# Input sums held back, keys between the norm's parts, MLP loads later and two of four weight sums on GpSimd, in a float32 hybrid decoder layer

## The chip, the cores and the metric

One core of a Trainium2 chip runs one launch. The metric is device time in microseconds; the kernel before took 1165.41 us, the median of three runs.

## The reference

One decoder layer in float32 over 1024 tokens of width 1024, cut to its computation:

```python
mod = silu(c) @ w_ada + b_ada
shift1, scale1, gate1, shift2, scale2, gate2 = split(mod, 6)
h = rms_norm(x) * (1 + scale1) + shift1
gq, gk, gv, g_lr, g_gate, hq, hf, hi, h_gate = split(h @ w_in)
# four GLA heads, four HGRN2 heads, causal, chunks of 64 tokens:
#   o_t = q_t S_t,  S_t = diag(exp(log_a_t)) S_{t-1} + k_t^T v_t
o_gla  = rms_norm(gla(gq, gk, gv, log_sigmoid(g_lr @ w2 + b2) / 16), g1) * silu(g_gate)
forget = lb + (1 - lb) * sigmoid(hf)
o_hgrn = rms_norm(gla(silu(hq), 1 - forget, hi, log(forget)), g2) * silu(h_gate)
x = x + gate1 * (concat(o_gla, o_hgrn) @ w_out)
h = rms_norm(x) * (1 + scale2) + shift2
x = x + gate2 * (square(relu(h @ w_mlp1)) @ w_mlp2)
out = rms_norm(x, final_norm_g)
```

## The kernel before

Each engine's program is one list of instructions, and semaphores order them across engines; nothing is scheduled at run time. Every large product is split in two parts for accuracy: an operand and a weight each have a high part (`ACT.Copy` to `fp32r`, on ScalarE) and a low part (value less high part, on GpSimd or VectorE), and TensorE makes high x high, high x low and low x high: twelve 128x512 matmuls for four tiles of depth.

The stages in order: the norm and modulation of `x`; projections of the head groups `P0`, `P1` and `H0`, one unit of 128 columns after another; then four long groups (`two_pairs`), which hold the remaining heads; the output projection (sixteen units, `out_unit`); the MLP, by a Strassen-like scheme with seven products; the last norm.

**A pair.** The four long groups make their projections in pairs, eight in all (`p` = 0 to 7, two to a group, "early" and "late"). A pair is two units of 128 columns by two halves of the tokens, made with seven products in place of eight. Six are `pair_product` (L1981), P1, P2, P6, P5, P4, P3 in TensorE's order. The seventh, P7, is cut in four pieces (`seventh_piece`, L2010), since its operand t3 is read back from DRAM in pieces: `piece_x` for pieces 0 and 2, `piece_y` for 1 and 3. Between the products stand the steps of the recurrence of the head before (`attend(n)`, from `attention_steps`): "k" and "v" transposes, "sc" scores, "up" state updates, "o" outputs, "ss" sums of squares. ScalarE copies keys out of PSUM (`keys`, L1329) and squares the outputs (`output`, L1334).

**Weights of a pair.** Four quarters `pq` of 256 KB come by DMA. Four sums of quarters are needed: S3 (for P7), S2 (for P6, in place on `pq[0]`), S1 (for P5) and S4 (for P3). VectorE makes all four (`weight_sum_of`, L2599 to L2619). ScalarE makes the high parts (`pair_high`, L1307) and GpSimd the low parts (`pair_low`, L965), in the order P1, P7, P2, P6, P5, P4, P3. Two products share one place in SBUF: P5 takes P1's, P4 P2's, P3 P6's. The next pair's quarters are loaded when S1, S4 and certain low parts are made (`load_pair_quarter`, L722). SP issues all DMAs in one order; a wait there holds all behind it.

**Operands of a pair.** Four sums of input blocks (`xs`, 2048 columns each, `add_parts` L2408, `subtract` L2414) are made on VectorE in `group` for `H0`, with high parts on ScalarE (`t1_hi`, `t4_hi` L1305) and low parts on VectorE or GpSimd (`low_fourth` L2430, L979).

**Bookkeeping of results.** `join` (L2623 to L2646) adds parts of the products into the banks that hold a quarter of the pair; `silu_of`, `gate_half`, `tanh_of` and `value_of` make the nonlinear steps of it. In `paired` the new head's decays go through a chain of VectorE and ScalarE: scan, k_rel, k_end (L2749, L2751), decay, q_cum (L2760), q_rel (L2763). `low_squares` (L2686) makes the low part of the squares, on which "ss" waits.

**Orders around the change.** The order in each engine's list is written by hand. The list of TensorE for a group:

```python
pair_product(early, P1); seventh_piece(early, 0); attend(0)
pair_product(early, P2); attend(1); pair_product(early, P6)
```

In ScalarE's list the transposes of the values ("v", at the start of the next group) depend on `value_of(0, late, "21")`, which stands near the end of `paired`, behind `norm_log(1)`, `norm_exp(1)` and the high parts P7 and P2 of the next pair. At the end of the groups SP loads `w_out` (`load_out`), the residual `x` (`load_x_back`, four DMAs of 1 MB) and the first MLP quarters (`load_quarter`).

## Time and profile before

| | |
|---|---|
| median of three runs | 1165.41 us (1165.19 to 1165.82) |
| the profiled execution's own time | 1166.44 us |
| its span | 1164.7 us |
| mean granted TensorE clock | 0.993 of full speed |
| TensorE busy | 1137.4 us, 98% |
| VectorE, ScalarE, GpSimd busy | 876.3, 612.9, 499.4 us (75%, 53%, 43%) |
| the four long groups | 224.9 to 440.5 us |
| HBM read, written | 138.51 MB, 40.89 MB |

Times in the rows are counted from the start of the span. PE is TensorE, DVE VectorE, ACT ScalarE, POOL GpSimd, SPq the DMA queue of SyncE. Matmuls are pipelined, so a matmul's own duration (0.39 us) is longer than the distance from one start to the next. What stands in brackets at the end of a row is the idle time ahead of the instruction and what ended it.

### The profile page before, as it was taken

Reading aid. Unit: us, or ns where it says so; the run is one execution under the profiler, and the core shown is the slowest. Engines: PE = TensorE matmul, PEld = TensorE weight load, DVE = VectorE, ACT = ScalarE, POOL = GpSimd, SP = SyncE. Lnnn points to the kernel's source line nnn. Section 1 sums busy time; section 2 is a strip of 40 time slices with the busy share of each in tenths; the row PEclk is TensorE's granted clock in tenths of the full one; section 3 lists DMA queues with packets and bytes.
Section 4 is the critical chain, followed back from the end, with each engine's and each line's share of the span. In section 5 each row is a group of like instructions: output and inputs, shape, how many; then the busy total and the mean of one; then the engine's idle time right before and its main releaser. Section 6 shows DMA issues by size and latency. Waiting matters only on the chain.

```text
span 1164.7 us, 15675 instructions
## 1 busy us (share of the span) xinstructions
PE 1137.4 (98%) x5555; PEld 939.3 (81%) x5555; DVE 876.3 (75%) x1048; ACT 612.9 (53%) x933; POOL 499.4 (43%) x318
## 2 busy tenths in 40 slices
PE   7999999899999999999999999999999999999996
PEld 6788788787878787888888888888888888788885
DVE  6898888877777677477976765677795884966776
ACT  7763564756566566345654555455664433424424
POOL 1021111534243344427534353344466675666741
PEclk9999999999999999999999999999999999999999
DMA  9777353044353549421455344544624637447203
GB/s 359 259 235 271 128 175 97 1 127 129 93 177 98 154 123 295 143 93 73 137 170 181 136 155 135 181 144 157 194 64 159 223 91 264 147 132 279 72 1 145
DMA packets 160549, 180.44 MB, mean 155 GB/s; under 512 B 7508, under 2 KB 119256, under 8 KB 157784
## 3 DMA queue, kind: packets, MB, share of 16 engines
q1 hardware_dynamic: 160472, 179.44, 46.4%
q8 instruction: 45, 0.74, 0.3%
q14 instruction: 32, 0.26, 0.1%
HBM read 138.51 MB, written 40.89 MB: 154 GB/s over the span
## 4 chain that ended last, share of the span: by engine, by line
PE 89%; DVE 4%; DMA 2%; ACT 2%; issue 1%; SPq 1%; POOL 1%; DVEq 0%; ACTq 0%
PE unit_bank L1742 16%; PE unit_bank L2156 9%; PE unit_bank L2158 9%; PE unit_bank L2157 9%; PE small_bank L2156 9%; PE small_bank L2158 9%; PE small_bank L2157 9%; PE unit_bank L2003 3%; PE small_bank L1742 3%; PE unit_bank L2005 3%; PE unit_bank L2004 3%; PE small_bank L1879 2%; DVE ada_acc L2257 1%; PE small_bank L1781 1%; DMA ada_slot<-in_w_ada_dram 1%
## 5 line engine op out<-in xcount | busy, mean ns | idle before, releaser
L997 POOL TENSOR_TENSOR wr_lo<-quarter,wr_hi 128x512 fp32r<-128x512 f32 x122 | 197.6, 1632 | 174.4 <-ACT wr_hi L1530 174.3
L2156 PE MATMUL unit_bank<-op_hi,wr_hi 128*128 128x512 f32 x452 | 176.5, 390 | 1.1 <-issue 1.1
L2158 PE MATMUL unit_bank<-op_hi,wr_lo 128*128 128x512 f32 x452 | 175.9, 389 | 0.0
L2157 PE MATMUL unit_bank<-op_lo,wr_hi 128*128 128x512 f32 x452 | 175.9, 389 | 0.0
L2156 PE MATMUL small_bank<-op_hi,wr_hi 128*128 128x512 f32 x448 | 174.5, 390 | 0.0
L2158 PE MATMUL small_bank<-op_hi,wr_lo 128*128 128x512 f32 x448 | 174.3, 389 | 0.0
L2157 PE MATMUL small_bank<-op_lo,wr_hi 128*128 128x512 f32 x448 | 174.3, 389 | 0.0
L1530 ACT ACTIVATE wr_hi<-wr_full 128x512 fp32r<-128x512 f32 x90 | 56.8, 631 | 173.3 <-DVE wr_full L2903 173.3
L2903 DVE TENSOR_TENSOR wr_full<-quarter,quarter 128x512 f32<-128x512 f32 x90 | 88.9, 989 | 56.3 <-PE small_bank L2158 23.0
L1530 ACT ACTIVATE wr_hi<-quarter 128x512 fp32r<-128x512 f32 x136 | 83.0, 626 | 90.5 <-PE unit_bank L2158 48.4
L1742 PE MATMUL unit_bank<-a_hi,w_hi 128*128 128x512 f32 x304 | 121.2, 399 | 0.8 <-DVE w_lo L2401 0.8
L1742 PE MATMUL unit_bank<-a_lo,w_hi 128*128 128x512 f32 x304 | 118.5, 390 | 0.0
L1742 PE MATMUL unit_bank<-a_hi,w_lo 128*128 128x512 f32 x304 | 118.4, 390 | 0.0
L997 POOL TENSOR_TENSOR wr_lo<-wr_full,wr_hi 128x512 fp32r<-128x512 f32 x48 | 80.2, 1673 | 77.0 <-ACT wr_hi L1530 65.6
L2156 PEld LDWEIGHTS unit_bank<-op_hi,wr_hi 128*128 128x128 f32 x452 | 84.8, 188 | 19.5 <-issue 2.1
L2157 PEld LDWEIGHTS unit_bank<-op_lo,wr_hi 128*128 128x128 f32 x452 | 84.9, 188 | 17.8 <-issue 0.2
L2158 PEld LDWEIGHTS unit_bank<-op_hi,wr_lo 128*128 128x128 f32 x452 | 84.8, 188 | 17.7
L2158 PEld LDWEIGHTS small_bank<-op_hi,wr_lo 128*128 128x128 f32 x448 | 84.1, 188 | 17.6
L2156 PEld LDWEIGHTS small_bank<-op_hi,wr_hi 128*128 128x128 f32 x448 | 84.1, 188 | 17.4 <-POOL wr_lo L997 0.2
L2157 PEld LDWEIGHTS small_bank<-op_lo,wr_hi 128*128 128x128 f32 x448 | 84.1, 188 | 17.4
L930 POOL TENSOR_TENSOR w_lo<-raw,w_hi 128x1024 fp32r<-128x1024 f32 x11 | 28.8, 2614 | 150.8 <-ACT w_hi L1054 150.8
L972 POOL TENSOR_TENSOR pw_lo<-pw_full,pw_hi 128x512 fp32r<-128x512 f32 x24 | 39.7, 1654 | 85.7 <-ACT pw_hi L1315 68.9
(366 smaller groups left out, 2397.2 us busy)
## 6 DMA issues: line engine op xcount, KB each, us to landing
quarter<-in_w_mlp_dram SPq DMA_DIRECT2D x128, 256.0 KB, 4.1
hidden_scratch<-hid SPq DMA_DIRECT2D x98, 256.0 KB, 2.4
ada_slot<-in_w_ada_dram SPq DMA_DIRECT2D x48, 512.0 KB, 6.1
op_full<-hidden_scratch SPq DMA_DIRECT2D x21, 1024.0 KB, 4.8
pair_quarter<-in_w_in_dram SPq DMA_DIRECT2D x32, 256.0 KB, 3.7
piece_x<-t_scratch SPq DMA_DIRECT2D x16, 512.0 KB, 4.1
piece_y<-t_scratch SPq DMA_DIRECT2D x32, 256.0 KB, 3.3
raw<-in_w_out_dram SPq DMA_DIRECT2D x16, 512.0 KB, 4.5
```

The lines of the kernel that those rows point to most:

```text
L930: pool.tensor_tensor(w_lo[slot][:, :, :], raw[slot][:, :, :], w_hi[slot][:, :, :].bitcast(F32), ALU.subtract).then_inc(wlo_ready, 1)
L972: pool.tensor_tensor(pw_lo[place][:, :, :], pair_source(prod), pw_hi[place][:, :, :].bitcast(F32), ALU.subtract).then_inc(pair_lo, 1)
L997: pool.tensor_tensor(wr_lo[slot][:, :, :], split_source(n), wr_hi[slot][:, :, :].bitcast(F32), ALU.subtract).then_inc(wr_lo_pool, 1)
L1530: act.activation(wr_hi[slot][:, :, :], split_source(n), ACT.Copy).then_inc(wr_hi_ready, 1)
L1742: return pe.matmul(out_ap, left, right, start=start, stop=stop)
L2003: pe.matmul(dst, wh, hi[:, k, :], start=k == 0 and prod not in (P6, P3), stop=False, skip_group_check=True)
L2004: pe.matmul(dst, wh, lo[:, k, :], start=False, stop=False, skip_group_check=True)
L2005: mm = pe.matmul(dst, wl, hi[:, k, :], start=False, stop=k == KH - 1, skip_group_check=True)
L2156: pe.matmul(dst, wh, ah, start=opens, stop=False, skip_group_check=True)
L2157: pe.matmul(dst, wh, al, start=False, stop=False, skip_group_check=True)
L2158: mm = pe.matmul(dst, wl, ah, start=False, stop=k == KH - 1, skip_group_check=True)
L2903: dve.tensor_tensor(dst[:, :, :], a[:, :, :], b[:, :, :], op).then_inc(w_sum, 1)
```

## The change

- VectorE makes S3 and S2 alone. GpSimd makes S1 just ahead of the low part of P5 and S4 just ahead of that of P3 (`late_weight_sum`), and counts them on a semaphore of their own, `late_sum`; ScalarE's high parts and SP's loads wait for that.
- In `H0`, S2 stands ahead of the decay and q_cum, and the last input sum and difference (`add_parts(xs[2], 1, 0, 7)` and `subtract(..., 8)`) wait for the low part of P2.
- The second norm of `H0` is cut apart: logarithms ahead of the first pair's keys, exponentials behind its P6, the high part of t4 behind P5; VectorE applies it after the first join, and the gate follows `low_fourth`. In the first pair pieces 1 and 2 come behind P5, piece 3 behind P4.
- In all groups "ss" of the first half (`attend(5)`) moves from between P3 and P1 into P1, after half its matmuls; `sq_hi` is made ahead of the copy of the output; `low_squares(1)` moves ahead of the decay; the high part of P7 moves ahead of `norm_log(1)`, `value_of(0, ...)` ahead of the high part of P2.
- `piece_x` is loaded by two DMAs.
- `x` comes back in four separate steps between the loads of `w_out`, and the eight MLP quarters come behind out load 7 instead of 3.

```diff
-PAIR_SUMS = ("S3", "S2", "S1", "S4")
+PAIR_SUMS = ("S3", "S2")
+LATE_SUMS = ("S1", "S4")
 ...
 # SP
-                elif i == 2:
-                    sp.wait_ge(pair_sum, pair_sum_of(p - 1, "S1"))
+                elif i == 2:
+                    sp.wait_ge(late_sum, late_sum_of(p - 1, "S1"))
 ...
-            for i in range(2):
-                load_x_back(i)
-            for v in range(2, 4):
+            load_x_back(0, 0)
+            load_out(2)
+            load_x_back(1, 0)
+            for v in range(3, OUT_HALVES):
                 load_out(v)
-            sp.wait_ge(normed, before("ss", 7))
-            sp.wait_ge(seventh_done, SEVENTH_0 + 4 * PAIRS)
-            for i in range(4):
-                for pr in range(2):
-                    load_quarter(0, pr, i)
-            for v in range(4, OUT_HALVES):
-                load_out(v)
+                if v in (5, 6):
+                    load_x_back(v - 5, 1)
+                if v == 7:
+                    sp.wait_ge(normed, before("ss", 7))
+                    sp.wait_ge(seventh_done, SEVENTH_0 + 4 * PAIRS)
+                    for i in range(4):
+                        for pr in range(2):
+                            load_quarter(0, pr, i)
 ...
 # GpSimd
+            def late_weight_sum(p, prod):
+                wait_place(pool, p, prod)
+                i, j, op = {P5: (2, 3, ALU.add), P3: (1, 0, ALU.subtract)}[prod]
+                pool.wait_ge(pq_loaded[i], X_LOADED_0 + 16 * (p + 1))
+                if prod == P5:
+                    pool.wait_ge(pq_loaded[j], X_LOADED_0 + 16 * (p + 1))
+                else:
+                    pool.wait_ge(pair_sum, pair_sum_of(p, "S2"))
+                pool.tensor_tensor(pw_full[PAIR_PLACE[prod]][:, :, :], pq[i][:, :, :], pq[j][:, :, :], op).then_inc(late_sum, 1)
 ...
                 for prod in SPLIT_ORDER:
+                    if (p, prod) == (0, P5):
+                        pool.wait_ge(t_made, T_MADE_0 + 9)
+                    if prod in (P5, P3):
+                        late_weight_sum(p, prod)
                     pair_low(p, prod)
 ...
 # ScalarE, paired
+                else:
+                    first_logs()
+                    keys(0)
+                    copy_part(early, 0)
+                    pair_high(early, P6)
+                    first_exps()
+                    pair_high(early, P5)
+                    fourth_high()
 ...
                 value_of(1, late, "22")
+                pair_high(late + 1, P7)
                 norm_log(1)
                 norm_exp(1)
-                pair_high(late + 1, P7)
+                value_of(0, late, "21")
                 pair_high(late + 1, P2)
-                value_of(0, late, "21")
 ...
 # TensorE, two_pairs
                 pair_product(early, P3)
-                attend(5)
-                pair_product(late, P1)
+                pair_product(late, P1, lambda: attend(5))
 ...
 # VectorE, group H0 and paired
                 if own == "H":
-                    weight_sum_of(0, "S2")
+                    dve.wait_ge(pair_lo, PAIR_LO_0 + split_of(0, P2))
                     add_parts(xs[2], 1, 0, 7)
                     subtract(xs[2], xs[2], xs[3], 8)
 ...
-                weight_sum_of(early, "S1")
                 dve.wait_ge(decay_ready, gi)
                 join(early, "11")
+                if early == 0:
+                    first_norms()
                 states(0)
                 if early == 0:
                     low_fourth()
-                weight_sum_of(early, "S4")
+                    first_gate()
 ...
-                weight_sum_of(late, "S1")
                 norms(0)
 ...
                 join(late, "11")
+                low_squares(1)
 ...
-                weight_sum_of(late, "S4")
-                low_squares(1)
                 join(late, "u")
```

## Rows read from the trace of the kernel before

**Rows 1.** Page, part 1 and the engines' shares of the chain in part 4

```profile
PE 1137.4 (98%) x5555; PEld 939.3 (81%) x5555; DVE 876.3 (75%) x1048; ACT 612.9 (53%) x933; POOL 499.4 (43%) x318
...
PE 89%; DVE 4%; DMA 2%; ACT 2%; issue 1%; SPq 1%; POOL 1%; DVEq 0%; ACTq 0%
```

**Rows 2.** TensorE's waits: total us, times, longest

```profile
PE small_bank L1742 <- DVE sq_lo L2686: 3.8, 6, 0.9
PE unit_bank L2003 <- POOL pw_lo L972: 1.9, 1, 1.9
...
PE unit_bank L2023 <- POOL pw_lo L972: 0.8, 1, 0.8
PE unit_bank L1742 <- DVE w_lo L2401: 0.8, 1, 0.8
```

**Rows 3.** Stretches: length, busy us of PE, PEld, DVE, ACT, POOL, clock, DMA, GB/s

```profile
229.00:232.00 3.00, 1.13 (x8) 0.72 (x7) 1.80 (x1) 2.96 (x5) 2.92 (x1) 0.87 0.00 0
...
234.00:236.00 2.00, 2.00 (x7) 1.52 (x6) 1.97 (x2) 2.00 (x4) 0.76 (x1) 0.50 0.57 132
```

**Rows 4.** Timeline of TensorE and ScalarE, first pair: start, us, instruction

```profile
231.98 0.80 PE L2003 MATMUL unit_bank<-a_hi,pw_hi 128*128 128x512 f32 x1 [1.87 <-POOL pw_lo L972]
...
237.40 1.46 PE L1742 MATMUL small_bank<-v_nat,k_nat 64*128 64x128 f32 x16
...
235.07 0.57 ACT L1329 ACTIVATE k_nat<-small_bank 128x512 f32<-128x512 f32 x1
```

**Rows 5.** Timeline of GpSimd and VectorE, first pair

```profile
225.40 3.26 POOL L972 TENSOR_TENSOR pw_lo<-pw_full,pw_hi 128x512 fp32r<-128x512 f32 x1 [2.73 <-DVE pair_quarter L2619]
228.62 3.31 POOL L972 TENSOR_TENSOR pw_lo<-pair_quarter,pw_hi 128x512 fp32r<-128x512 f32 x1
...
225.24 2.29 DVE L2408 TENSOR_TENSOR x_sum<-a_hi,a_lo 128x2048 f32<-128x2048 f32 x1
227.56 3.25 DVE L2414 TENSOR_TENSOR x_sum<-x_sum,x_sum 128x2048 f32<-128x2048 f32 x1
```

**Rows 6.** Timeline of GpSimd and VectorE, late pair of the second group

```profile
322.00 3.00 POOL L972 TENSOR_TENSOR pw_lo<-pw_full,pw_hi 128x512 fp32r<-128x512 f32 x1 [5.34 <-ACT pw_hi L1315]
324.96 1.30 POOL L972 TENSOR_TENSOR pw_lo<-pair_quarter,pw_hi 128x512 fp32r<-128x512 f32 x1
...
322.64 1.22 DVE L2751 TENSOR_TENSOR k_end<-k_end,t 128x1024 f32<-128x1024 f32 x1
...
325.07 2.27 DVE L2760 SCALAR_TENSOR_TENSOR q_cum<-q_rel,q_cum 128x1024 f32<-128x1024 f32 x1
327.45 1.23 DVE L2763 SCALAR_TENSOR_TENSOR q_rel<-q_rel,t 128x1024 f32<-128x1024 f32 x1
328.60 0.68 DVE L2619 TENSOR_TENSOR pw_full<-pair_quarter,pair_quarter 128x512 f32<-128x512 f32 x1
```

**Rows 7.** Timeline to the next group's first transposes: VectorE, ScalarE, TensorE

```profile
332.51 0.68 DVE L2619 TENSOR_TENSOR pw_full<-pair_quarter,pair_quarter 128x512 f32<-128x512 f32 x1
...
333.35 1.28 ACT L1345 ACT_TABLE_LOAD   x1
...
338.22 0.58 ACT L1378 ACTIVATE vT<-unit_bank 128x512 f32<-128x512 f32 x1
...
330.03 0.47 PE L1742 MATMUL small_bank<-sq_hi,ones 128*128 128x512 f32 x1 [0.95 <-DVE sq_lo L2686]
...
338.94 0.74 PE L1781 MATMUL small_bank<-ident,vT 128*128 128x128 f32 x5
```

**Rows 8.** Timeline in the MLP, VectorE and GpSimd

```profile
578.23 1.67 DVE L2903 TENSOR_TENSOR quarter<-quarter,wr_full 128x512 f32<-128x512 f32 x1
...
577.74 1.60 POOL L1017 TENSOR_TENSOR hid<-hid,hid 128x512 f32<-128x512 f32 x1 [2.02 <-DVE hid L3024]
```

**Rows 9.** Chain in order of time (start, us, piece) and ScalarE's timeline, end of attention

```profile
452.46 38.42 PE unit_bank L1742 x168
...
450.09 1.06 ACT L1074 ACTIVATE w_hi<-raw 128x1024 fp32r<-128x1024 f32 x1 [2.45 <-DMA raw<-in_w_out_dram]
```

More of the change, by code:

```diff
@@ L760, in load_mixed_back, with load_x_back @@
                 sp.dma_start(mixed[:, 0, :], mixed_dram).then_inc(mixed_back, 16)
-            def load_x_back(i):
+            def load_x_back(i, half):
                 sp.wait_ge(six_done, six_of(PAIRS - 1, P4 if i else P5))
-                for half in range(2):
-                    part = slice(half * HALF, (half + 1) * HALF)
-                    sp.dma_start(xT[:, 4 * i:4 * i + 4, part], x_dram[:, 4 * i:4 * i + 4, part]).then_inc(x_back[i][half], 16)
+                part = slice(half * HALF, (half + 1) * HALF)
+                sp.dma_start(xT[:, 4 * i:4 * i + 4, part], x_dram[:, 4 * i:4 * i + 4, part]).then_inc(x_back[i][half], 16)
             def load_out(v):
@@ L1301, in group, with first_logs, first_exps, fourth_high @@
                     read_out(7, "v")
-                    read_out(7, "ss")
-                    act.wait_ge(t_done, T_DONE_0 + 1)
-                    act.wait_ge(t_made, T_MADE_0 + 9)
-                    act.activation(t4_hi[:, :, :], xs[2][:, :, :], ACT.Copy).then_inc(t_high, 1)
+            def first_logs():
+                for which in range(2):
+                    act.wait_ge(filled["ss"], before("ss", 2) + 2 + which + 1)
+                    act.activation(stat[:, which, :], SB[2 + which][:, :], ACT.Ln, bias=eps, scale=1.0 / P
+                                   ).then_inc(read["ss"], 1)
+            def first_exps():
+                for which in range(2):
+                    act.wait_ge(read["ss"], before("ss", 2) + 2 + which + 1)
+                    act.activation(stat[:, which, :], stat[:, which, :], ACT.Exp, scale=-0.5).then_inc(o_rms, 1)
+            def fourth_high():
+                act.wait_ge(t_done, T_DONE_0 + 1)
+                act.wait_ge(t_made, T_MADE_0 + 9)
+                act.activation(t4_hi[:, :, :], xs[2][:, :, :], ACT.Copy).then_inc(t_high, 1)
             def pair_high(p, prod):
@@ L2005, in pair_product @@
                     mm = pe.matmul(dst, wl, hi[:, k, :], start=False, stop=k == KH - 1, skip_group_check=True)
+                    if between and k == 1:
+                        between()
                 mm.then_inc(six_done, 1)
@@ L2502, in both_read @@
                         dve.wait_ge(unit_read[half], u + 1)
-                def gate(u, n, head, half=None, place=None):
-                    th, xx = (t0[:, :], t1[:, :]) if half is None else (tok(t0, place), tok(t1, place))
-                    for hf in (0, 1) if half is None else (half,):
-                        dve.wait_ge(unit_read[hf], u + 1)
-                    dve.scalar_tensor_tensor(th, th, 1.0, xx, ALU.add, ALU.mult).then_inc(gate_silu, 1)
-                    dve.wait_ge(gate_silu, n + 1)
-                    dve.wait_ge(normed, before("ss", gi) + (half + 1 if half is not None and head == 7 else 0))
-                    dst = row(mixed, head) if half is None else tok(row(mixed, head), half)
-                    dve.scalar_tensor_tensor(dst, th, 0.5, dst, ALU.mult, ALU.mult).then_inc(gated, 1)
                 u0 = 4 * gi + 1
@@ L2580, in group @@
                 read_out(6)
+                if own == "H":
+                    weight_sum_of(0, "S2")
                 if prev:
@@ L2591, in group, with first_norms @@
                 if own == "H":
-                    weight_sum_of(0, "S2")
+                    dve.wait_ge(pair_lo, PAIR_LO_0 + split_of(0, P2))
                     add_parts(xs[2], 1, 0, 7)
                     subtract(xs[2], xs[2], xs[3], 8)
-                read_out(7)
+                if own == "P":
+                    read_out(7)
                 if name == "P0":
                     then(dve.memset(masked[:, :, :], 0.0))
-                if own == "H":
-                    gate(u0 + 3, hh, hh)
+            def first_norms():
+                for which in range(2):
+                    dve.wait_ge(o_rms, before("ss", 2) + 2 + which + 1)
+                    dst = tok(mixed[:, 2 + which], 1)
+                    dve.scalar_tensor_tensor(dst, dst, cols[:, R_GG:R_GG + 1], stat[:, which, :], ALU.mult, ALU.mult
+                                             ).then_inc(normed, 1)
@@ L2601, in weight_sum_of, with first_gate @@
+            def first_gate():
+                for half in range(2):
+                    dve.wait_ge(unit_read[half], 13)
+                dve.scalar_tensor_tensor(t0[:, :], t0[:, :], 1.0, t1[:, :], ALU.add, ALU.mult).then_inc(gate_silu, 1)
+                dve.wait_ge(gate_silu, 1)
+                dve.wait_ge(normed, before("ss", 2))
+                dve.scalar_tensor_tensor(mixed[:, 0], t0[:, :], 0.5, mixed[:, 0], ALU.mult, ALU.mult).then_inc(gated, 1)
             def weight_sum_of(p, kind):
+                dve.wait_ge(pq_loaded[2 if kind == "S3" else 3], X_LOADED_0 + 16 * (p + 1))
@@ L2611, in weight_sum_of @@
[L2611 to L2619 removed]
+                    wait_place(dve, p, P7)
@@ L2795, in gates @@
                 gate_quarter(t0, 0, early, "11", 5, 0, 13)
-                weight_sum_of(early, "S4")
                 masks(0)
```

73 lines of the change are left out of this document (35 added, 38 removed).

## The prediction

> **What bounds the kernel now.** I read the page first: TensorE is busy for 1137.4 of 1164.7 us, 98%, and the chain that ended last lies on it for 89% [rows 1]. So a faster VectorE or ScalarE is worth only what TensorE waits for them. The table of TensorE's waits comes next, since it lists what can be won at all. The change aims at four of its lines [rows 2]: six waits for `sq_lo` (3.8 us), one each for `pw_lo` at L2003 (1.9) and L2023 (0.8), and one for `w_lo` (0.8). Together that is 7.3 us, and about 0.16 us more at each of the nine stops, because the first matmul after one runs long. The third view is the granted clock by stretch [rows 3]: 0.87 at 229 to 232 us, 0.50 after that. It is there because the waits at 228 and 230 us follow each other, and it makes them dearer than they look: between 231.98 and 237.40 stand the twelve matmuls of one product, 0.45 us apart [rows 4], where a stretch at the upper level (2.4 GHz) takes 0.23 each (38.42 us for 168) [rows 9]. That is 2.7 us more for the product. The fourth view, the timelines of VectorE and GpSimd, says what made the operands late.
>
> **Part 1, the sums of inputs held back, and the first norms.** GpSimd's `pw_lo` takes 1.30 us when left alone [rows 6] and 3.26 and 3.31 here, while VectorE runs sums of 2048 elements beside it [rows 5]. After the change S2 comes ahead of q_cum (0.6 us later for q_cum) and the large sums wait for both `pw_lo`. I put P7's at 225.3 to 226.6 and P2's at 226.6 to 227.8. Then both waits on `pw_lo` and the slow stretch go: 1.9 + 0.8 + 0.3 + 2.7 = 5.7 us. What is late next: before, the norms' logarithms and exponentials stood ahead of `keys` (ScalarE reads the keys out at 235.07) [rows 4]. Now the logarithms come first, then keys at about 231, then P6's high part, and its low part is there at about 233.9. TensorE asks for it at about 232.9: 1.0 us lost. The norms themselves are applied later too, at about 236.5, and SP's loads of the pieces queue behind that wait. The pieces 1 and 2 now come behind P5 to cover it; I take 0.6 us for what is left, and 0.4 for P5's sum on GpSimd. So TensorE ends the fourth quarter 3.7 us earlier. Not all of that reaches the next group: VectorE has `low_fourth` (2.3 us, as the sum at 225.24), the gate (two products of 1.2 us, as q_rel's) and the joins still to do, with two GpSimd sums between, and I put the chain through it at only 2.4 us earlier. Term: **-2.4**, bounds -5.7 (nothing late) and 0 (the clock falls at P6's wait as well).
>
> **Part 2, the squares.** Making `sq_hi` ahead of the copy of the output gives 0.5 us, the matmuls of the first half move 1.4 us into P1 (six matmuls at 0.23), and `low_squares(1)` moves up. All six waits for `sq_lo` go. In a group that makes TensorE about 1.7 us early at the end of the late pair: 0.95 us at 330.03 [rows 7] and the rest at the first half.
>
> **Part 3, two weight sums to GpSimd.** Here something comes back. A sum is 0.68 us on VectorE [rows 6]; on GpSimd I take 1.30, the price of a subtract of the same shape there. Sixteen of them are 21 us on an engine busy 43% of the time, so its busy time does not matter, but the place does. The two engines exclude each other: the `pw_lo` asked for at 322.00 takes 3.00 us while VectorE makes k_end, and q_cum takes 2.27 us against 1.23 for q_rel, of the same size [rows 6]. I follow the late pair of the second group. Without S1, k_rel starts 0.6 us earlier and k_end is done at 323.2. Then, one after the other: `pw_lo` of P5 and P4 to 325.7, `sq_lo` to 326.3, S4 on GpSimd to 327.6, q_cum to 328.75, `pw_lo` of P3 to 330.0, q_rel to 331.15. Before, q_rel ended at 328.68. So it is 2.5 us later, against 1.28 us (S4 and `sq_lo`) that VectorE no longer does behind it. S3 of the next pair starts at 332.51 before, 3.83 us after q_rel's end [rows 6, 7]; now 2.55 us after it and 0.4 behind a `pw_lo`: 334.1, done at 334.8.
>
> The change also puts P7's high part ahead of the second norm, so ScalarE waits for that S3. From there: 0.6 us for the high part, 3.83 for the logarithm and exponential with their two table loads (333.35 to 338.22 less two high parts of 0.52) [rows 7], and 0.72 from `value_of` to the transposes. They start at 340.0 instead of 338.94: **+1.0 us a group, three groups, +3.0**. TensorE is ready at 338.94 - 1.7 = 337.2 and stands still for 2.8 us. Bounds: if P3's `pw_lo` comes behind q_rel, q_rel ends at 329.9 and the transposes are 0.2 us early (-0.6 in all); if each `pw_lo` or sum loses one more round, +1.2 more a group. I take the value near the first, since GpSimd got the port at 578.1, in the 0.03 us between two sums of VectorE [rows 8]: the second took 1.67 us. The row that speaks the other way is 322.00, where GpSimd asked first and VectorE's next instruction still went ahead.
>
> The Trainium skill (SBUF — State Buffer, "Who interferes with whom") says that whoever issues first gets the pair of ports for the whole instruction. At 322.00 the trace does not agree. By the page P3's `pw_lo`, asked for at 328.3, goes ahead of q_rel, as I have it; by the row at 322.00 it would not, and the result is the rival below.
>
> **The clock.** It fell after waits of 0.81 and 1.87 us 1.4 us apart [rows 2, 3], and not after the waits of 0.95. A wait of 2.8 us lies beyond both. One fall costs 2.7 us where twelve matmuls and more run in it; some of the slow time falls into the wait, so I take 2.2, and two falls in three groups: **+4.4**. Bounds 0 and 8.1.
>
> **Part 4, loads at the end of attention.** The third `raw` lands behind 4 MB of `x`, its high part starts at 450.09 [rows 9] and TensorE waits 0.8 us for the low one. With only a quarter of `x` ahead it is early: **-0.9**. The eight quarters of the MLP go behind out load 7, at about 463 us, and are first read behind the sixteen output units (5.5 us each from 440.5, an estimate from [rows 9]: 528), so I cost them at nothing; were they late, it would be the 4 us of one load.
>
> The second DMA for each `piece_x` costs SP its issue, in a queue that waits for TensorE anyway: 0, bounds -0.4 and +0.4 in all.
>
> **Sum.** -2.4 + 3.0 + 4.4 - 0.9 = **+4.1 us**, with the waits for `sq_lo` already inside the +1.0. The profiled execution took 1166.44 us (span 1164.7 and 1.7 around it), 1.03 above the median of 1165.41; I apply the sum to the median: **1169.5 us**.
>
> **Rivals.** *Faster, the transposes in time:* P3's `pw_lo` comes behind q_rel, the wait at the transposes is 1.5 us and the clock stays up, as it did after 0.95. Then -3.7 for the first pair, -0.6 and -0.9: 1160.2 us; should the port never be contended in these places, each group gains another 0.8: 1157.8. For it: all of VectorE's work off its busiest stretch. Against it: S4 then is late as well, and the next pair's load with it. It decides at q_rel's end: before 329.9 this case, after 330.5 mine. *No change:* the transposes neither earlier nor later, one or two falls of the clock (3.3): -2.4 - 0.9 + 3.3 = 0, 1165.4. *Much slower:* the clock falls in all three groups and at P6 in the first pair, which then gives nothing: -0.9 + 3.0 + 8.1 = +10.2, 1175.6; I give it little, since P6's wait of 1.0 is near the 0.95 that held. *The change does not do what it says:* if the held sums make t4 late for P4, the first pair gives nothing: +2.4 on any case; the sum is done at 232.4 and needed at 244, so 3 in 100.
>
> **Chances.** Slower as forecast 0.43, much slower 0.03, no change 0.12, faster 0.42. A measurement of this kernel tells 0.2% (2.3 us) from nothing. The two large cases are of both signs. The forecast's own range is 1166.5 to 1173; over all cases 8 in 10 lie in 1157.0 to 1173.0.
>
> **What would show it.** Right: in the trace of after no wait for `sq_lo`, no `pw_lo` over 2.5 us at 225 to 228, granted clock 1.00 at 229 to 238; and in each late pair q_rel ending 2 us or more behind where it did against k_end, P7's high part waiting for S3, a wait of over 2 us at the transposes (L1781) for `vT`, and a stretch at 0.50 behind it. Wrong: waits at L1781 under 1 us and no 0.50 after 230 us; then the port was not where VectorE's time went, and the time is near 1160.

## The result, and the profile after

The kernel after takes 1183.1 us, the median of four runs (1180.64 to 1185.02), against 1165.62 for the kernel before on the same chip: a ratio of 1.0137, 95% interval 1.0113 to 1.0162. Forecast were 1169.5 and a range that ended at 1173.0. The direction was right, the loss four times as large as its sum. The profiled execution took 1180.64 us (span 1178.9, 14.2 longer than before).

The page of the kernel after, part 1 and the engines' shares of the chain in part 4:

```profile
PE 1141.9 (97%) x5555; PEld 944.7 (80%) x5555; DVE 872.4 (74%) x1032; ACT 612.9 (52%) x933; POOL 517.1 (44%) x334
...
PE 63%; DVE 1%; ACT 1%; DMA 0%; issue 0%; POOL 0%; DVEq 0%; ACTq 0%
```

The shares of the chain sum to 65%: it was not followed back over the rest of the span, so they can't be set beside [rows 1]. The same 5555 matmuls, 4.5 us more of busy time (the slow clock), and the rest is waiting. VectorE is less busy than in [rows 1], GpSimd, with sixteen more sums to make, 17.7 us more; neither share says that anything is wrong. The table of TensorE's waits does (columns: total us, times, longest), beside [rows 2]:

```profile
PE small_bank L1827 <- ACT vT L1416: 6.6, 3, 2.5
...
PE small_bank L1788 <- DVE masked L2716: 3.7, 1, 3.7
PE unit_bank L2071 <- POOL pw_lo L988: 3.5, 3, 1.2
PE unit_bank L2049 <- DVE unit_bank L2696: 3.0, 3, 1.2
```

Before, only the first of these four lines existed, with one wait of 0.3 us; the other three are new. Five of the six waits for `sq_lo` are gone (one of 0.97 us is left), and so are the two on `pw_lo` of 0.81 and 1.87 us. L1827 are the values' transposes, L2071 the first piece of P7 behind them, L2049 the product P3, L1788 the second scores of the first pair, whose bank VectorE must first have read for the masks of the first scores. The third line is an example of a releaser that was not it: the `pw_lo` that the piece needs, P7's, had ended at 346.48 us in the second group, and the piece started at 351.84. What ended just before is the silu of quarter 12 (351.05, 0.69 long), whose bank the piece writes. The windows of the kernel after show where the clock fell (columns: window, length, busy time and count of TensorE, weight load, VectorE, ScalarE, GpSimd, then the granted clock as a mean of the window, where 1.00 is 2.4 GHz and 0.50 is 1.2 GHz, DMA share and GB/s):

```profile
246.00:250.00 4.00, 1.95 (x9) 1.95 (x10) 2.56 (x3) 0.13 (x1) 0.28 (x1) 0.60 0.97 305
250.00:254.00 4.00, 4.00 (x12) 3.15 (x12) 0.00 (x0) 0.50 (x1) 1.27 (x1) 0.55 0.00 1
...
294.00:298.00 4.00, 3.36 (x10) 2.81 (x11) 1.23 (x2) 2.10 (x5) 2.65 (x3) 0.57 0.16 49
...
350.00:354.00 4.00, 2.85 (x19) 2.28 (x18) 1.76 (x3) 2.79 (x6) 2.68 (x3) 1.00 0.06 9
...
407.00:411.00 4.00, 3.18 (x10) 2.69 (x11) 1.38 (x2) 2.10 (x5) 2.75 (x3) 0.57 0.13 28
```

It fell three times, behind the masks and behind two of the three stops at the transposes; behind the third (2.13 and 1.15 us of waiting, as long as the others) it stayed up. All this is of one execution; the others of this kernel have no trace.

Cut at the start of pair 0 and at the transposes, the stretches of the four long groups are these; the last columns are the output projection, and the MLP up to the start of TensorE's last matmul (us, from the starts of TensorE's matmuls in the traces; the experiments are named as below):

| kernel | first | second | third | gates | output | MLP and end |
|---|---|---|---|---|---|---|
| before | 60.88 | 53.15 | 53.03 | 48.53 | 89.21 | 625.54 |
| after | 66.24 | 57.20 | 55.98 | 50.72 | 88.73 | 625.12 |
| a1, sums on VectorE | 62.41 | 54.71 | 54.56 | 49.42 | 88.10 | 624.66 |
| a2, high part behind norm | 64.44 | 52.88 | 53.01 | 48.90 | 88.74 | 624.91 |
| a3, masks first | 60.83 | 58.48 | 58.48 | 50.07 | 88.75 | 625.19 |
| a4, before and the two sums | 60.20 | 53.52 | 53.53 | 48.41 | 90.35 | 625.06 |
| b1, before and the order | 59.32 | 54.20 | 53.96 | 49.45 | 89.49 | 624.89 |
| b2, before and held sums | 63.52 | 53.61 | 53.56 | 48.52 | 89.30 | 624.65 |
| b3, before and squares | 60.11 | 53.98 | 54.06 | 49.95 | 88.35 | 625.17 |
| b4, before and loads | 60.68 | 53.16 | 53.29 | 48.58 | 88.11 | 625.21 |
| c1, low squares back | 67.24 | 55.27 | 55.31 | 48.87 | 88.79 | 625.47 |
| c2, both mended | 58.66 | 52.90 | 53.31 | 48.91 | 88.78 | 624.43 |
| c3, new order | 59.47 | 52.96 | 52.90 | 48.28 | 88.15 | 624.77 |
| c4, new order, held sums | 58.85 | 53.05 | 53.14 | 48.38 | 88.11 | 625.27 |

So 5.36 + 4.05 + 2.95 + 2.19 us were lost in the groups, and 0.9 won behind them. The rest of the 14.2 us lies outside the table: pair 0 starts 1.27 us later than before (in a3, with the same code up to there, 0.27), and behind the last matmul 0.75 us are won. The first column has luck of the clock in it. The same first pair, with the same waits of 0.8 and 1.87 us, takes 6.8 us from the start of P2 to that of P6 in before and b4, and 5.6 us in a4, b1 and c3, where the clock was back at 1.00 sooner. So 1.2 us of what these three seem to win in the first group belongs to no edit. Two places carry the loss.

**The first pair.** VectorE's timeline in the kernel after (columns: start us, duration, engine, line, operation; the idle time ahead in brackets):

```profile
235.76 1.83 DVE L2646 SCALAR_TENSOR_TENSOR mixed<-mixed,cols,stat 128x512 f32<-128x512 f32 x2 [1.47 <-ACT stat L1334]
237.51 3.02 DVE L2729 SCALAR_TENSOR_TENSOR state<-state,decay,small_bank 128x128 f32<-128x128 f32 x8
240.44 2.50 DVE L2482 TENSOR_TENSOR t_lo<-x_sum,t_hi 128x2048 fp32r<-128x2048 f32 x1
242.86 2.30 DVE L2653 SCALAR_TENSOR_TENSOR t<-t,t 128x1024 f32<-128x1024 f32 x1
245.19 2.17 DVE L2656 SCALAR_TENSOR_TENSOR mixed<-t,mixed 128x1024 f32<-128x1024 f32 x1
247.28 0.71 DVE L2716 COPY_PREDICATED masked<-causal,small_bank 128x512 f32<-128x512 uint32 x1
```

The norm, the recurrence's states, the low part of t4 and the gate now stand ahead of the masks in one list, and the gate's products take 2.30 and 2.17 us where q_rel's takes 1.23 in before: GpSimd's S4 runs beside the first (240.75 to 244.08) and its low part of P3 beside the second (244.88 to 246.29). Before, the norm and the gate were done by 236.2 (234.94 + 1.23) and the masks began at 244.69. TensorE waited from 244.4 to 248.05, and behind the stop, with the clock down, the eight matmuls of the scores took 1.73 us in place of 0.82 and the twelve of P4 4.77 in place of 2.98.

**The late pair.** The same place as [rows 6] and [rows 7], in the kernel after, VectorE:

```profile
331.30 1.22 DVE L2801 TENSOR_TENSOR k_end<-k_end,t 128x1024 f32<-128x1024 f32 x1
332.44 0.69 DVE L2696 TENSOR_TENSOR unit_bank<-unit_bank,k_nat 128x512 f32<-128x512 f32 x1
334.80 0.75 DVE L2736 TENSOR_TENSOR sq_lo<-stat,sq_hi 128x512 fp32r<-128x512 f32 x1 [1.67 <-ACT sq_hi L1378]
335.47 1.26 DVE L2806 COPY decay<-q_cum 128x16 f32<-128x16 f32 x1
336.76 1.23 DVE L2811 SCALAR_TENSOR_TENSOR q_cum<-q_rel,q_cum 128x1024 f32<-128x1024 f32 x1
338.10 2.12 DVE L2814 SCALAR_TENSOR_TENSOR q_rel<-q_rel,t 128x1024 f32<-128x1024 f32 x1
...
342.24 1.49 DVE L2752 SCALAR_TENSOR_TENSOR mixed<-t,mixed 128x512 f32<-128x512 f32 x1
343.64 0.68 DVE L2669 TENSOR_TENSOR pw_full<-pair_quarter,pair_quarter 128x512 f32<-128x512 f32 x1
```

and ScalarE:

```profile
340.25 0.60 ACT L1406 ACTIVATE t<-unit_bank 128x512 f32<-128x512 f32 x1 [2.83 <-DVE q_rel L2814]
341.17 0.63 ACT L1353 ACTIVATE pw_hi<-pair_quarter 128x512 fp32r<-128x512 f32 x1 [0.32 <-DMA pair_quarter<-in_w_in_dram]
341.71 0.60 ACT L1416 ACTIVATE vT<-unit_bank 128x512 f32<-128x512 f32 x1
344.42 0.63 ACT L1353 ACTIVATE pw_hi<-pw_full 128x512 fp32r<-128x512 f32 x1 [2.11 <-DVE pw_full L2669]
345.07 1.28 ACT L1383 ACT_TABLE_LOAD   x1
...
348.90 0.58 ACT L1416 ACTIVATE vT<-unit_bank 128x512 f32<-128x512 f32 x1
```

VectorE is idle 1.67 us for the high squares, the decay of 16 columns takes 1.26 us, q_rel 2.12, the gate's half 1.49. Then ScalarE waits 2.11 us for S3 (made at 343.64), because P7's high part is ahead of the norm. From k_end's start to q_rel's end it is 8.92 us where before took 6.04. The values come at 348.90 + 0.58, and the second norm, the join and the silu of quarter 12, which stand behind it, later still.

### The profile page after: what moved, and what is told of

The parts are those of the page before. It is cut to its first block, busy times and chain, and to the rows that moved or that the text cites. A ratio compares the mean times of both kernels' runs of the same rounds, so it can differ in the third digit from the quotient of the medians.

```text
span 1178.9 us, 15692 instructions
## 1 busy us (share of the span) xinstructions
PE 1141.9 (97%) x5555; PEld 944.7 (80%) x5555; DVE 872.4 (74%) x1032; ACT 612.9 (52%) x933; POOL 517.1 (44%) x334
## 4 chain that ended last, share of the span: by engine, by line
PE 63%; DVE 1%; ACT 1%; DMA 0%; issue 0%; POOL 0%; DVEq 0%; ACTq 0%
PE unit_bank L2208 9%; PE unit_bank L2210 9%; PE unit_bank L2209 9%; PE small_bank L2210 9%; PE small_bank L2208 9%; PE small_bank L2209 9%; PE unit_bank L1788 7%; PE unit_bank L2049 1%; PE unit_bank L2051 1%; PE unit_bank L2050 1%; PE small_bank L1788 1%; DMA mixed<-mixed_scratch 0%; PE small_bank L1925 0%; PE unit_bank L2217 0%; PE small_bank L2217 0%
## 5 line engine op out<-in xcount | busy, mean ns | idle before, releaser
L1788 PE MATMUL unit_bank<-a_hi,w_hi 128*128 128x512 f32 x304 | 121.3, 399 | 0.0
L1788 PE MATMUL unit_bank<-a_lo,w_hi 128*128 128x512 f32 x304 | 118.7, 390 | 0.0
L1788 PE MATMUL unit_bank<-a_hi,w_lo 128*128 128x512 f32 x304 | 118.7, 390 | 0.0
L2209 PEld LDWEIGHTS unit_bank<-op_lo,wr_hi 128*128 128x128 f32 x452 | 84.8, 188 | 17.7 <-issue 0.2
L2209 PEld LDWEIGHTS small_bank<-op_lo,wr_hi 128*128 128x128 f32 x448 | 84.2, 188 | 17.5
L2208 PEld LDWEIGHTS small_bank<-op_hi,wr_hi 128*128 128x128 f32 x448 | 84.0, 188 | 17.5 <-POOL wr_lo L1017 0.2
L988 POOL TENSOR_TENSOR pw_lo<-pair_quarter,pw_hi 128x512 fp32r<-128x512 f32 x32 | 42.4, 1328 | 63.2 <-ACT pw_hi L1353 63.2
```

The costliest lines, as they stand in the source:

```text
L988: pool.tensor_tensor(pw_lo[place][:, :, :], pair_source(prod), pw_hi[place][:, :, :].bitcast(F32), ALU.subtract).then_inc(pair_lo, 1)
L1788: return pe.matmul(out_ap, left, right, start=start, stop=stop)
L2208: pe.matmul(dst, wh, ah, start=opens, stop=False, skip_group_check=True)
L2209: pe.matmul(dst, wh, al, start=False, stop=False, skip_group_check=True)
```

## The experiments

Theories: P, the two sums on GpSimd make the late pair late; O, P7's high part ahead of the second norm does; V, VectorE's wait for the high squares does; G, the order in the first pair costs what the waits on `pw_lo` had cost, and more. Each was undone alone, and the part of the change that it belongs to was done alone on the kernel before; the loads (Part 4) were only done alone.

### Undone in the kernel after

**a1**, S1 and S4 on VectorE again:

```diff
+                late_weight_sum(early, P5)
                 dve.wait_ge(decay_ready, gi)
...
-                    if prod in (P5, P3):
-                        late_weight_sum(p, prod)
                     pair_low(p, prod)
```

> The kernel after, but VectorE makes S1 and S4 again, at the places they have in the kernel before. Theory P (the two sums on GpSimd are what makes the late pair late): q_rel ends 5 to 6 us after k_end's start where it was 8.9, the waits at the values' transposes (2.0, 2.1, 2.5 us), at P3's join (1.2, 0.9, 0.9) and at the first piece (1.15 three times) go, with the two falls of the clock behind them: about 12 + 3, so 1168 us. Theory O (it is P7's high part ahead of the second norm): the waits at the transposes and at the first piece keep at least 2 us a group, time 1176 or more. Both: the first pair keeps its wait of 3.7 us for the masks.

Measured: 1170.68 us, ratio 1.0035 (1.0022 to 1.0048); 12.4 us of the 17.5 come back. But neither the waits nor their sizes came out as P had them:

```profile
PE unit_bank L2056 <- POOL pw_lo L977: 3.5, 3, 1.2
PE small_bank L1812 <- ACT vT L1401: 3.4, 3, 1.1
...
PE small_bank L1773 <- DVE masked L2712: 1.5, 1, 1.5
```

The wait at the transposes halves (6.6 to 3.4), the one at the first piece stays, the one at P3 shrinks to 0.32 us (0.91 to 1.15 in the kernel after). The clock stayed at 1.00 behind all three stops at the transposes, so a part of the 12.4 us is the clock's. So the sums are a part of it, not the whole. The masks come earlier too, since the gate no longer shares the ports with a GpSimd sum: its products take 1.21 and 1.23 us there, in place of 2.30 and 2.17.

**a2**, P7's high part behind the norm again:

```diff
-                pair_high(late + 1, P7)
                 norm_log(1)
                 norm_exp(1)
+                pair_high(late + 1, P7)
                 value_of(0, late, "21")
```

> The kernel after, but P7's high part stands behind the norm's logarithm and exponential again, sums still on GpSimd. Theory O: ScalarE no longer waits 2.1 us for S3, the values come 2.1 us earlier, the second norm and all behind it (join, tanh, silu of quarter 12, first piece) too: wait at the transposes 0 to 0.3, at the first piece 0, P3's join still 0.9; 3 x 3.2 us and two falls of the clock (about 3 us) less: 1170 us. Theory P: the stop only moves to the low part of P7 or stays, time within 3 us of the kernel after, 1180.

Measured: 1169.73 us, 1.0032 (1.0018 to 1.0045), 13.4 us less, as O has it (1170). One line moved gives back three quarters of the loss, with both sums still on GpSimd and q_rel as late as before the edit:

```profile
334.38 2.12 DVE L2814 SCALAR_TENSOR_TENSOR q_rel<-q_rel,t 128x1024 f32<-128x1024 f32 x1
...
338.61 1.28 ACT L1383 ACT_TABLE_LOAD   x1
339.92 0.68 DVE L2669 TENSOR_TENSOR pw_full<-pair_quarter,pair_quarter 128x512 f32<-128x512 f32 x1
...
342.96 0.58 ACT L1416 ACTIVATE vT<-unit_bank 128x512 f32<-128x512 f32 x1
```

Here k_end starts at 327.59, and q_rel ends 8.91 us later. S3 is made beside the norm's logarithm, so nothing waits for it, and from S3's start to the transposes it is 3.77 us where the kernel after has 5.98. The second and third group take 52.88 and 53.01 us, as much as before (53.15 and 53.03). So P's "only moved" is out: with this order q_rel's lateness costs these groups nothing on balance. The details of O are not all right: the first piece still waits 0.63 us and P3 0.90, and they stand where before waited 0.3 to 0.4 and 0.9 us for the squares. The clock stayed at 1.00 in the late pairs, and the stop for the masks is still there (2.75 us).

**a3**, the masks first in the first pair:

```diff
+                masks(0)
                 if early == 0:
                     low_fourth()
-                    first_gate()
-                masks(0)
                 silu_of(q_rel, 0, early, "11", made + 1)
+                if early == 0:
+                    first_gate()
```

> The kernel after, but in the first pair VectorE makes the first masks ahead of the low part of t4, and the gate behind the silu of q. If the 3.7 us wait and the fall of the clock behind it come from the gate and the low part standing ahead of the masks: both go, 3.7 and 1.9 us for P4's twelve matmuls, so 5.6 us less than after: 1177. Rival: the wait is only passed on, to the low part of t4 (2.5 us, needed by P4) or to the joins behind the gate: less than 2 us gained, 1181. In both the late pairs of the three groups stay as they are.

Measured: 1176.78 us (1173.02 to 1179.62), 1.0091 (1.0069 to 1.0113), 6.3 us less, as the first expectation has it (1177). The first group falls from 66.24 to 60.83, and the wait for the masks is gone; a wait of 1.9 us for the low squares takes a part of its place. The second and third group took 58.48 each in this profile, with a slow stretch in each, where the kernel after has 57.20 and 55.98 with one.

**c1**, the low squares behind q_rel again:

```diff
                 join(late, "11")
-                low_squares(1)
                 dve.wait_ge(read["up"], before("chunks", gi + 1))
...
+                low_squares(1)
                 join(late, "u")
```

> The kernel after, but the low squares of the second half behind q_rel again. Theory V (VectorE's wait of 1.67 us for the high squares, ahead of the decay, q_cum and q_rel, is a part of the lateness): q_rel ends 1.5 to 2.4 us earlier, the wait at the transposes falls from 2.2 to under 1 us, one or two falls of the clock fewer: 1173 to 1177. Rival (GpSimd's works fill that stretch anyway and VectorE then waits for the port instead): q_rel less than 0.7 us earlier, 1180 or more.

Measured: 1175.8 us, 1.0082 (1.0065 to 1.0100), 7.3 us less. V's numbers come true: q_rel ends 7.01 us after k_end's start where the kernel after had 8.92, and no wait at the transposes is left. Its reason does not. The low squares behind q_rel take 1.75 us, in the second group S3 starts 12.23 us after k_end's start (12.34 in the kernel after), ScalarE waits for it as long as there, and the values' last copy starts 17.49 us after k_end's start (17.60):

```profile
342.05 0.63 ACT L1353 ACTIVATE pw_hi<-pw_full 128x512 fp32r<-128x512 f32 x1 [2.12 <-DVE pw_full L2669]
```

The transposes find their values ready because TensorE is itself later, stopped ahead of them at `sq_lo` for up to 2.7 us, longer than ever before:

```profile
PE small_bank L1788 <- DVE sq_lo L2736: 8.6, 4, 2.7
...
PE small_bank L1788 <- DVE masked L2716: 3.7, 1, 3.7
```

Behind these stops the clock fell in all three groups (0.67 at 337 to 341 us in the second), so "one or two falls fewer" is missed. One stop takes the place of those at P3 and at the transposes, and at most 0.63 us are left at the first piece: the second and third group take 55.27 and 55.31 us.

**c2**, a2 and a3 together:

> The kernel after with two repairs, P7's high part behind the norm and the first masks ahead of the low part of t4. If the two losses are separate they add: 13.4 us and 6.3 us less than after, 1163.4 us, faster than before. If TensorE's earlier arrival in the first group only finds the next late operand (the low squares of the first half, 1.9 us where the masks came first alone), 1166 to 1168.

Measured: 1163.07 us (nine runs), 0.9978 (0.9969 to 0.9988). Apart they gave 13.4 and 6.3 us, together 20.0: two separate losses, and without them the change is a gain of 2.8 us (the loads alone gain 1.4, b4). The wait for the low squares in the first pair stays (1.70 us).

### Done alone on the kernel before

**a4**, the two sums on GpSimd (`late_weight_sum`, its semaphore and waits, as in the diff above):

> The kernel before with only the two sums S1 and S4 moved to GpSimd. Theory P: q_rel ends some 2 us later against k_end, the transposes wait 1 to 1.5 us in three groups, 0 or 1 fall of the clock: 1169 to 1172. Theory O: with P7's high part behind the norm ScalarE has the slack, the transposes wait under 0.5 us: 1165 to 1166. If GpSimd's port share is the whole matter, over 1175.

Measured: 1167.02 us (ten runs), 1.0012 (1.0003 to 1.0022). P's number is missed, and so is O's (1165 to 1166), by 1.0 us; the transposes do not wait at all. The stop is another:

```profile
PE small_bank L1767 <- DVE sq_lo L2711: 6.1, 6, 1.7
```

The low squares now cost TensorE 1.73 us in each late pair, where before had 0.93 to 0.95. The second and third group take 0.37 and 0.50 us more. The four stretches sum to 215.66 us against 215.59, but only since the first has the 1.2 us of the clock's luck: without it, it would be 0.5 longer too. The output projection takes 1.14 us more, and its waits on low parts grow (0.75 to 1.27 us, and a new one of 0.50). GpSimd starts `a_lo` there 0.7 us later (434.18 against 433.47), and `load_out` now waits for GpSimd's sums; which of the two is the cause is not shown. From k_end to q_rel's end it is 7.00 us, but k_end starts 0.9 us earlier in the group.

**b1**, the order of ScalarE's list:

```diff
+                pair_high(late + 1, P7)
                 norm_log(1)
                 norm_exp(1)
-                pair_high(late + 1, P7)
+                value_of(0, late, "21")
                 pair_high(late + 1, P2)
-                value_of(0, late, "21")
```

> The kernel before with one edit: P7's high part ahead of the second norm (and the second value's copy ahead of P2's high part). Theory O (this order alone costs, whoever makes the sums): ScalarE finishes the first value at 333.33 and the next S3 is made at 332.51 to 333.19 there, so it waits 0 to 0.1 us, the norm starts 0.6 us later, and the values 0.1 us later or, with P2's high part behind them, 0.4 earlier: time within 1 us of 1166. Theory I (order and late S3 together cost; each alone little): the same number. Theory R (the order is the whole loss): the transposes wait over 1 us and the time is over 1170.

Measured: 1168.38 us (ten runs), 1.0022 (1.0011 to 1.0032), outside the 1 us that was expected. ScalarE does not wait for S3 here, and the values are in time:

```profile
332.77 0.58 ACT L1378 ACTIVATE vT<-unit_bank 128x512 f32<-128x512 f32 x1
333.24 0.62 ACT L1315 ACTIVATE pw_hi<-pw_full 128x512 fp32r<-128x512 f32 x1
...
337.72 0.58 ACT L1378 ACTIVATE vT<-unit_bank 128x512 f32<-128x512 f32 x1
338.19 0.62 ACT L1315 ACTIVATE pw_hi<-pair_quarter 128x512 fp32r<-128x512 f32 x1
339.24 0.60 ACT L1368 ACTIVATE t<-unit_bank 128x512 f32<-128x512 f32 x1 [0.42 <-DVE unit_bank L2646]
```

But the tanh of quarter 12 still comes at 339.24, behind the norm on VectorE and its join, and the first piece waits 1.15, 1.15 and 1.04 us for it. The second and third group and the gates take 1.05, 0.93 and 0.92 us more; the first 1.56 less, of it 1.2 the clock's luck. I had looked at the transposes and not at what TensorE asks for next.

**b2**, Part 1 alone (the edits of `H0`, `paired` and `two_pairs` from the diff, and the two DMAs per `piece_x`):

> The kernel before with Part 1 alone (held sums, first norm cut, gate behind the low part of t4, piece order; two DMAs per piece_x). As forecast on record: 2.4 us less, 1163. Theory G (the gate and the low part stand ahead of the masks, TensorE waits 1.5 to 3.7 us there, and the clock may fall): the first group takes 61.5 to 63 us where before took 60.9, 1167 to 1168.

Measured: 1168.22 us (ten runs), 1.0020 (1.0009 to 1.0030): 2.4 us more where 2.4 less was on record, just above G's 1167 to 1168. But G's place is not the main one. Both waits on `pw_lo` at 228 and 232 us are gone as said, and from pair 0's start to its P3 it takes 27.14 us where before took 29.10: up to there the part is the gain that was forecast. The group still takes 63.52 us. Its stops are 1.20 at P6, 1.25 at a piece (probably since the norm's wait holds SP's list), only 0.83 at the masks, where G has 1.5 to 3.7, and

```profile
258.72 0.47 PE L1772 MATMUL small_bank<-sq_hi,ones 128*128 128x512 f32 x1 [3.17 <-DVE sq_lo L2732]
```

3.17 for the first low squares. VectorE is not behind there (idle 0.98 and 0.49 us just before them); it waits for the high squares, which ScalarE makes at 256.70. They are the eighth of the instructions that ScalarE could start only at 253.26, when the weight sum S3 was made. In the kernel after the same place costs 0.97 us and the masks 3.68: the gate's products take 1.21 and 1.23 us here and 2.30 and 2.17 there, beside GpSimd.

**b3**, Part 2 alone (`sq_hi` ahead of the copy, `attend(5)` inside P1, `low_squares(1)` ahead of the decay):

> The kernel before with Part 2 alone (high squares ahead of the copy, sums of squares inside P1, low squares ahead of the decay). If nothing else binds, the six waits for sq_lo (3.8 us) go: 1162. Theory V (VectorE now waits some 1.7 us for the high squares ahead of the decay and q_cum, so that q_rel, the values and the transposes come later): TensorE's wait only moves to the transposes, 1165 to 1167.

Measured: 1169.28 us (nine runs), 1.0029 (1.0018 to 1.0039). This is above V's range (1165 to 1167), and V has the mechanism. Every wait for `sq_lo` in the groups is gone, and more comes back at the transposes:

```profile
324.39 1.28 DVE L2687 TENSOR_TENSOR sq_lo<-stat,sq_hi 128x512 fp32r<-128x512 f32 x1 [1.07 <-ACT sq_hi L1340]
```

```profile
PE small_bank L1781 <- ACT vT L1378: 4.9, 3, 1.7
```

TensorE's 0.95 us at the squares becomes 1.65 at the transposes. The second and third group take 0.8 and 1.0 us more and the gates 1.4. The first takes 0.8 less: the clock did not fall in its first pair, in this execution.

**b4**, Part 4 alone (the two hunks of SP's loads):

> The kernel before with Part 4 alone (x back in four steps, MLP quarters behind out load 7). As forecast: the wait of 0.75 us for w_lo at 452.5 goes, 0.9 us less, 1165.1. Rival: another wait takes its place in the same stage (first_w_lo, a_lo): 1166.

Measured: 1164.39 us (ten runs), 0.9987 (0.9977 to 0.9996). As forecast (1165.1), within the interval: no wait for `w_lo` is left, and 1.1 us of the gain lies in the output projection (88.11 against 89.21).

### A version from it

**c3**, the kernel before with Part 4, the high squares ahead of the copy and `attend(5)` inside P1 but the low squares where they were, b1's order, and this against b1's new wait:

```diff
                 value_of(0, late, "21")
+                tanh_of(t0, 1, late, "12")
                 pair_high(late + 1, P2)
-                tanh_of(t0, 1, late, "12")
...
                 join(late, "21")
+                join(late, "12")
                 norms(1)
-                join(late, "12")
```

> The kernel before with Part 4, the high squares ahead of the copy and the sums of squares inside P1 (low squares where they were), P7's high part ahead of the norm, and the join of quarter 12 ahead of the norm with its tanh ahead of P2's high part. Theory C (a chain on VectorE and ScalarE, S3 to norm to values and quarter 12, sets the groups' pace together with TensorE): with silu of quarter 12 about 1.3 us earlier than in the kernel with the order alone, the wait at the first piece (1.15 us, three times) goes, groups of 52.2 to 52.9 us where before took 53.1: 1162. Rival: the groups stay at 53.1, since q_rel is no earlier: 1164.4, as with Part 4 alone.

Measured: 1163.12 us (nine runs), 0.9980 (0.9970 to 0.9989), between C's number and the rival's. The waits at the first piece are gone, but the second and third group gain only 0.1 to 0.2 us: TensorE now waits 1.26 us for the second low squares, at each late pair. About 1.4 of the 2.7 us won are the loads' (b4).

**c4**, the same with the held sums, and the masks ahead of the low part of t4:

> The same with Part 1 as well, masks ahead of the low part of t4 and the gate behind silu of q; all four sums on VectorE. If the waits on pw_lo at 228 and 230 us (5.7 us with the slow clock) go and the first group's VectorE work fits: 58 us for the first group where before took 60.9, 1159 us. Rival: VectorE's backlog makes the low squares of the first half 2 to 3 us late and the group takes 60.5 or more: 1162.

Measured: 1162.18 us (seven runs, 1161.72 to 1162.85), 0.9970 (0.9960 to 0.9981), the lowest median here and better than both kernels; its interval overlaps with those of c2 and c3. The first group takes 58.85 us, 2.0 less than before but only 0.6 less than c3, and not the 58 of the expectation: 1.19 us at P6 and 1.10 at the low squares stay.

## Why the forecast was wrong

It said slower, by the right place and with the right first half of the mechanism, and put +4.1 us where +14.2 in the profiles (17.5 between medians) were measured.

**Part 1, -2.4: the first step that failed.** The waits on `pw_lo` and their slow stretch did go. The forecast then put "the chain through it at only 2.4 us earlier", by naming VectorE's low part, gate and joins as still to do without placing them one behind another up to the next thing that TensorE asks for. That is the masks, and on VectorE's list they stand behind 11.5 us of work (235.76 to 247.28), of which the gate is needed by nothing near and the low part of t4 only by P4, behind the masks. TensorE stood still 3.68 us there. From pair 0's start to its P3 it takes 31.48 us in the kernel after and 29.10 in before: +2.4 where -2.4 stood. Putting the masks first gives 6.3 back (a3), the fall of the clock included. Alone the part costs 2.4 us too (b2), but there the stop that costs it is the one behind the masks, at the low squares. P6's wait was right (1.0 forecast, 0.90 measured), and I gave the case that this stop also costs the clock 3 in 100; the clock fell at the masks, which were in no case.

**Part 3, +1.0 a group: the second step, and the dearer one.** Less the first pair's 2.4, and less 2.5 for the clock (below), the groups lost 9.7 us where +3.0 stood. The chain was right, and two terms of it are missing. q_rel's end was to come 9.1 us after k_end's start (331.15 less 322.04, S1 being gone), measured 8.92; S3 to transposes 5.9, measured 5.98; the wait at the transposes 2.8, measured 1.95 to 2.48. In the third group, which had no slow stretch, the loss is 2.95 us. Split at k_end, q_rel and S3, and set against before: 0.59 up to k_end's start (forecast -0.6), 2.86 up to q_rel's end, -0.06 up to S3 (forecast -0.9; the gate's half took 1.49 us beside a `pw_lo`), -0.44 behind it. The first missing term is the 1.15 us at the first piece; the norm's lateness reaches it through quarter 12, 2 us behind the point where I stopped. The second is the 0.8 us at S3.

**Whose it is: the attribution failed too.** I charged the sums on GpSimd, at +3.0 for three groups. Alone they cost 1.0 us in all (a4). The order of ScalarE's list costs 2.6 us alone, Part 2 with the low squares' place 3.5 (b3), the held sums 2.4, the loads win 1.4: that is 8.1 together, and the change costs 17.5. The rest is their interplay. With any one of the three taken back (a1, a2, c1), 7 to 13 us return. For the two larger ones the traces show how. In the second group, from k_end's start (us):

| kernel | S3 starts | the values' last copy starts |
|---|---|---|
| before; b1, the order; b3, the squares | 9.87; 10.15; 10.36 | 15.58; 15.65; 16.38 |
| a1, the order and the squares | 10.62 | 16.07 |
| a4, the sums | 12.27 | 15.81 |
| a2, the sums and the squares | 12.33 | 15.37 |
| c1, the sums and the order | 12.23 | 17.49 |
| after, all three | 12.34 | 17.60 |

The sums on GpSimd make S3 some 2 us late, whatever the rest. That costs the values nothing while P7's high part stands behind the norm, and the order costs them nothing while S3 is early: in b1 it is made at 332.91 and asked for at 333.24, 0.3 us to spare. Only both together make ScalarE wait for S3, and the norm, the values and quarter 12 wait with it. The low squares' place adds 0.4 to 0.8 us where VectorE makes the sums (a1 against b1, b3 against before) and 0.1 in the kernel after (against c1), so the 7.3 us that come back in c1 do not come from earlier values. As the forecast mentioned the move of P7's high part, and followed it, it had the parts; but it took them as one sum against the present order and never asked what each would be without the others.

**The clock, +4.4.** Two falls in the late pairs were forecast, two came. Their price was 1.2 us (second group against third) and 1.3 (gates against b1's, which have nearly the same wait at the first piece), 2.5 in all for 4.4. That it was two is of this execution: a3's shows three. The third, at the masks, cost 2.7 (0.9 on the scores and 1.8 on P4).

**Part 4, -0.9:** b4 shows -1.4 (0.5 to 2.7), of it 1.1 in the stage named. In the kernel after the stage wins 0.5, with a new wait of 0.49 us for a low part. **Part 2:** "all six waits for `sq_lo` go" was nearly so, five of six; that it costs VectorE a wait of 1.07 to 1.67 us ahead of q_rel was inside the chain that I followed (`sq_lo` to 326.3) but charged to GpSimd's ports.

**The rule on the ports.** The forecast weighed the Trainium skill (SBUF — State Buffer, "Who interferes with whom": whoever issues first gets the pair) against the row at 322.00. The Trainium skill says this there of VectorE's modes that use both pairs of ports; of an instruction with two inputs in SBUF, as k_end, it says that it contends with GpSimd's reads, and of all that the order of issue decides. The pattern of 322.00 came back: GpSimd asks at 331.28, while k_rel runs (330.17 to 331.39), k_end is issued behind it and still goes ahead at its usual 1.22 us, and the `pw_lo` takes 2.40 against 1.30 alone. The Trainium skill and these rows differ, as far as the starts in the trace tell the order of asking. With P3's `pw_lo`, asked for at 337.50 while q_cum ran, GpSimd did go ahead, and q_rel took 2.12 us, as by the Trainium skill; so it did at 240.75, ahead of the gate's first product. What decides between the two is not shown. The sequence of the forecast held through the whole late pair; what it lacked lay behind it.

## What to carry to other kernels

When an edit lets an engine be early, follow the other engines' lists in their written order to each thing that it asks for next, and further than the first: here two stops were found at the masks and at the piece 2 us behind the forecast one. An order can hold by 0.3 us of slack; before a wait is put ahead of a long chain (a high part ahead of a norm, a low part ahead of q_rel), see by how much its operand is early, in this change's timing and not in the old one. And try a change of several parts part by part: only the loads were a gain alone, and two small moves in the lists stand between a loss of 17 us and a gain of 3.

## What the runs showed that was not expected

- A stop does not decide by its length whether the clock falls: 2.13 and 1.15 us of waiting at 349.6 and 351.8 left it at 1.00, the same pair of waits of 1.95 and 1.15 at 292.4 and 294.6 brought it to 0.57 (windows above). In before, waits of 0.81 and 1.87 us in the first pair brought it to 0.50 [rows 3]; in b3 the same pair, 0.80 and 1.87 us, at 228.31 and 231.58, left it at 1.00:

```profile
232.00:234.00 2.00, 2.00 (x11) 1.62 (x10) 2.00 (x3) 2.00 (x2) 0.00 (x0) 1.00 0.00 0
```

So a stretch of one trace against that of another can differ by 1 to 3 us with no edit behind it.
- A copy of 16 columns takes 1.26 us (VectorE at 335.47), while GpSimd's S4 runs until 336.69, and 0.17 in b3 (at 325.59), where GpSimd is idle: here the price of sharing is the rest of the other engine's instruction, however small one's own is.
- A sum of two quarters on GpSimd takes 1.27 to 1.29 us alone, nearly as the subtract that stood in for it (1.30), and 1.74 to 3.33 beside VectorE's large instructions.
